# Two feed-forward layers on one NeuronCore: the second products as seven block products too

## What is computed

```
def hybrid_layer(...):            # first block, its last lines
    ...
    x + rms_norm(square(relu(rms_norm(x, g_pre_mlp) @ w_ff1)) @ w_ff2, g_post_mlp)

def swiglu(h, w1, w2):            # second block
    gt, up = jnp.split(h @ w1, 2, axis=-1)
    return (jax.nn.silu(gt) * up) @ w2
...
    h = rms_norm(x, norm_ffn_pre[l])
    x = x + rms_norm(swiglu(h, w_ffn_in[l], w_ffn_out[l]), norm_ffn_post[l])
```

## Time and profile before

| | us |
|---|---|
| median of 3 runs | 3385.32 (3380.46 to 3385.62) |
| the profiled execution's own time | 3380.83 |
| its span, first to last instruction | 3378.7 |
| TensorE busy | 3280.3 (97%) |
| VectorE busy | 1656.5 (49%) |
| ScalarE busy | 1066.0 (32%) |
| GpSimd busy | 1133.3 (34%) |
| chain that ended last, on TensorE | 85% of the span |

### The profile page before, as it was taken

How to read it: one execution, slowest core, us unless ns; L and a number is a source line. 1 busy time by engine, 2 the same in 40 slices (tenths; PEclk the granted TensorE clock), 3 DMA queues, 4 the chain that set the end, 5 groups by cost and what they waited for, 6 DMA issues and landing times.

```text
span 3378.7 us, 39689 instructions
## 1 busy us (share of the span) xinstructions
PE 3280.3 (97%) x15800; PEld 2669.5 (79%) x15800; DVE 1656.5 (49%) x2048; ACT 1066.0 (32%) x1479; POOL 1133.3 (34%) x667
## 2 busy tenths in 40 slices
PE   8999999999999999999999999999999999999997
PEld 6788777877876888788868778777778678887886
DVE  6752455435327675322153337563563577776213
ACT  3212444444324333211133333312343432223112
POOL 2112222212341554233322124341245345554325
PEclk9999999999999999999999999999999999999998
DMA  3545434316413223322224224224254222224223
GB/s 132 162 103 155 126 132 163 105 66 228 152 60 113 107 106 142 120 100 97 97 106 144 91 75 140 78 69 148 97 203 152 81 80 83 76 93 145 100 75 124
DMA packets 117198, 390.66 MB, mean 116 GB/s; under 512 B 13648, under 2 KB 23248, under 8 KB 116880
## 3 DMA queue, kind: packets, MB, share of 16 engines
q1 hardware_dynamic: 115984, 384.58, 33.3%
q10 hardware_dynamic: 1040, 3.67, 0.3%
HBM read 277.37 MB, written 113.84 MB: 116 GB/s over the span
## 4 chain that ended last, share of the span: by engine, by line
PE 85%; DVE 8%; issue 2%; ACT 2%; DMA 2%; POOL 1%; SPq 0%; DVEq 0%; POOLq 0%; ACTq 0%
PE pair L324 54%; PE pair L2145 16%; PE pair L443 4%; PE wide L834 2%; PE bank L654 2%; PE bank L802 2%; PE wide L567 1%; DVE act_lo L557 1%; DVE s_tmp L960 1%; POOL w_lo L2111 0%; PE wide L1513 0%; DVE p L625 0%; DMA proj<-p 0%; PE bank L1513 0%; DVE s_state L960 0%
## 5 line engine op out<-in xcount | busy, mean ns | idle before, releaser
L285 POOL TENSOR_TENSOR w_lo<-w_raw,w_hi 128x1024 fp32r<-128x1024 f32 (+1 forms) x240 | 564.8, 2358 | 1753.5 <-ACT w_hi L281 1712.8
L324 PE MATMUL pair<-act_hi,w_hi 128*128 128x512 f32 x2336 | 747.8, 401 | 10.4 <-DVE f1v L2170 6.1
L324 PE MATMUL pair<-act_lo,w_hi 128*128 128x512 f32 x2336 | 723.1, 391 | 0.0
L324 PE MATMUL pair<-act_hi,w_lo 128*128 128x512 f32 x2336 | 721.7, 390 | 0.0
L324 PEld LDWEIGHTS pair<-act_lo,w_hi 128*128 128x128 f32 x2336 | 439.2, 188 | 94.6
L324 PEld LDWEIGHTS pair<-act_hi,w_lo 128*128 128x128 f32 x2336 | 438.7, 188 | 94.7
L281 ACT CAST w_hi<-w_raw 128x1024 fp32r<-128x1024 f32 x210 | 220.7, 1051 | 909.9 <-PE pair L324 850.5
L324 PEld LDWEIGHTS pair<-act_hi,w_hi 128*128 128x128 f32 x2336 | 418.6, 189 | 92.0 <-issue 10.1
L625 DVE TENSOR_TENSOR p<-pair,rs 128x1024 f32<-128x1024 f32 x100 | 122.2, 1222 | 390.7 <-PE pair L324 390.6
L2298 DVE TENSOR_TENSOR f1acc<-f1acc,pair 128x1024 f32<-128x1024 f32 (+1 forms) x22 | 26.9, 1221 | 193.3 <-PE pair L324 193.3
L2111 POOL TENSOR_TENSOR w_lo<-w_raw,w_hi 128x512 fp32r<-128x512 f32 x64 | 98.7, 1544 | 60.2 <-ACT w_hi L2110 60.1
(11 more groups left out here) (627 smaller groups left out, 6192.8 us busy)
## 6 DMA issues: line engine op xcount, KB each, us to landing
w_raw<-in_stream SPq DMA_DIRECT2D x275, 512.0 KB, 3.6
proj<-p SPq DMA_DIRECT2D x101, 512.0 KB, 2.6
hidden<-f1v SPq DMA_DIRECT2D x32, 512.0 KB, 2.6
m2g<-proj SPq DMA_DIRECT2D x32, 512.0 KB, 5.0
act_lo<-hidden SPq DMA_DIRECT2D x24, 512.0 KB, 6.8
hidden<-f2v SPq DMA_DIRECT2D x22, 512.0 KB, 2.6
m1g<-proj SPq DMA_DIRECT2D x16, 512.0 KB, 3.5
f1hl<-hidden SPq DMA_DIRECT2D x16, 512.0 KB, 6.8
```

The lines of the kernel that those rows point to most:

```text
L285: last = nc.gpsimd.tensor_tensor(wlo[:, slot, at:at + n], raw[:, slot, at:at + n], whi[:, slot, at:at + n].bitcast(F32), ALU.subtract)
L324: last = nc.tensor.matmul(out_pair[:, h * HALF:(h + 1) * HALF], wt, a[:, h * HALF:(h + 1) * HALF], start=k == 0 and n_pass == 0, stop=k == ...
```

## The change

The second products are done in pairs of seven block products too, but for the last two output tiles of each layer. A pair of a second product is one of the four pairs of output tiles (i = 0 to 3) by one group of hidden tiles; the first layer gets 15 such pairs, the second 11 (the three of its last group have block products of 3 tiles, 9 matmuls, where the others have 12). The first products get one more pair in each layer, since only two units run plainly ahead of them, not four.

A block product takes one of eight "roles" of the activations: four are sums T1 to T4, four are plain blocks. For the hidden activations, `half_sums_of` makes the four sums on VectorE in SBUF for two hidden tiles at a time while the first product runs, and stores them to new DRAM buffers (`sums1`, `sums2`). At a change of group, each role is loaded into the place of the same role of the old group as soon as the last pair of the old group is through with it (`load_role`), in two pieces (j = 0 and 1) of two tiles each, 128x1024. `split_role` splits them: both high parts by ScalarE copies, the low part of piece 0 by VectorE, that of piece 1 by GpSimd. Roles 0 to 2 are split in the last three products of the old group's last pair, roles 3 to 6 in the first four products of the new group's first pair.

The seven products of a pair run in one order everywhere. Their results are summed in PSUM: ScalarE copies bank a into bank b ahead of product 2 and bank b into bank c ahead of product 4 (`seeds`), and the matmuls of products 2 to 6 accumulate onto what stands in their bank. The sums of weight blocks go to PSUM (`w_sum`), and four of the seven low parts of weights are VectorE's work now (`w_low`), three stay with GpSimd.

The diff's core ("..." marks what is left out):

```diff
-        pairs = pairs_in_all - 3
+        pairs = pairs_in_all - 2
...
-        S1, S2, S3, S4 = sq[:, H0], sq[:, H1], squares[:, H0], squares[:, H1]
+        sum_at = {4: wide[:, H0], 2: wide[:, H1], 1: bank[0][:], 6: bank[1][:]}
...
+        def weights_at(q, step):
...
+            elif step == 2:
+                w_high(q, 0)
+                w_low(q, 0)
+                w_sum(q, 1)
+                w_high(q, 1)
+            elif step == 3:
+                w_low(q, 1)
+                w_sum(q, 4)
+                w_sum(q, 2)
+                w_high(q, 2)
+                w_high(q, 3)
+                w_low(q, 3)
+            elif step == 4:
+                w_low(q, 2)
+                w_sum(q, 6)
+                w_high(q, 4)
...
+        def seeds(q, p):
+            if p == 0:
+                a_to_b[q] = A.mark(A.after(done[q, 0], b_read[q - 1] if q else entered[2]).copy(b, a))
+            elif p == 2:
+                b_to_c[q] = A.mark(A.after(done[q, 2], c_read[q - 1] if q else entered[1]).copy(c, b))
...
+        def outer(q, p):
...
+            if p == 1:
...
+                d_mid[q] = into(r1[:, H1], d, 1, True)
+            elif p == 2:
+                V.after(b_to_c[q])
+                b_read[q] = into(r1[:, H0], b, 2, True)
+            elif p == 3:
+                a_read[q] = into(r0[:, H0], a, 3, True)
+            elif p == 4:
+                c_mid[q] = into(r1[:, H1], c, 4, False)
...
+        def split_role(g, n, mark=None):
...
+            for j in range(2):
...
+                m = A.mark(A.after(here[g, n, j], mark).copy(hi, src))
+                on = G if j else V
+                role_ready[g, n, j] = on.mark(on.after(m).tensor_tensor(lo, src, hi.bitcast(F32), ALU.subtract))
...
+            for p in range(7):
+                product(q, p)
+                seeds(q, p)
+                if changing is not None and p not in waiting:
+                    load_role(changing, p, done[q, p])
...
+                (inner if q < pairs else outer)(q, p)
...
+                if changing is not None:
+                    if p > 3:
+                        split_role(changing, p - 4)
+                if opened is not None and p < 4:
+                    split_role(opened, p + 3, done[q - 1, 6])
...
+                if q < last:
+                    weights_at(q + 1, p)
...
+        PE.after(a_read[last], b_read[last], c_read[last], d_read[last])
```

More of the change, by code:

```diff
@@ L2016, in mlp @@
-        weights, sums = {}, {}
+            b_ready[i, k] = V.mark(V.after(high).tensor_tensor(operand(hl, (i,), k), t_src[i](k),
+                                                               operand(hh, (i,), k).bitcast(F32), ALU.subtract))
+        first = base + 2
+        n_groups = len(groups)
+        total = pairs + 4 * n_groups - 1
+        last = total - 1
+        first_m = [sum(groups[:g]) // 2 for g in range(n_groups)]
+        a, b, c, d = (pair[at][:, half] for at in range(2) for half in (H0, H1))
@@ new lines, in w_fetch @@
+        def w_fetch(q):
+            for n in range(2):
+                u = first + 2 * q + n
+                fetch_unit(u + 2, u % 2)
+        def weights_at(q, step):
+            if step == 0 and q > 1:
+                w_low(q - 1, 6)
+            elif step == 2:
[14 more added lines that the diff above has]
+                w_high(q, 4)
+            elif step == 5:
+                w_low(q, 4)
+                w_high(q, 5)
+                w_low(q, 5)
+                G.then(sums_of[q, 6])
+                nc.gpsimd.sem_inc(s_split, 2)
+                nc.scalar.sem_inc(s_whi, 2)
+            elif step == 6:
+                w_high(q, 6)
+                w_fetch(q)
@@ L2054, in mlp @@
         for k in range(4):
[L2055 to L2069 removed]
+            t_low(T2, k, high[T2, k])
@@ new lines, in outer, with into @@
+        def outer(q, p):
+            g, i = group_of(q), (q - pairs) % 4
+            r0, r1 = y[:, 2 * i, :], y[:, 2 * i + 1, :]
+            def into(dst, psum, n, fresh):
+                V.after(done[q, n])
+                if fresh and g == 0:
+                    return V.mark(nc.vector.tensor_copy(dst, psum))
+                return V.mark(V.then().tensor_tensor(dst, dst, psum, ALU.add))
+            if p == 1:
+                if g == 0 and i == 1:
+                    V.after(*(s.last() for s in hid_out))
+                if g == 0 and i == 3:
+                    V.after(hid_sum.last())
+                d_mid[q] = into(r1[:, H1], d, 1, True)
```

612 lines of the change are left out of this document (346 added, 266 removed).

## The result

| | before | after |
|---|---|---|
| median | 3382.91 us (7 runs) | 3394.68 us (7 runs, 3393.15 to 3397.26) |
| ratio to before | | 1.0037, 95% interval 1.0025 to 1.0048 |
| span of the profiled execution | 3378.7 us | 3391.8 us |
| granted clock of TensorE, mean | 0.993 | 0.984 |

The account below looks back on a forecast made before the run. TensorE, busy 97% of the span, bounds the kernel through its number of matmuls. 3380.8 - 74.1 (matmuls) - 31 (stops) + 81 (changes) + 8 (entries) + 2 + 2 (ends) = 3368.7, stated as 3370 us; range 3312 to 3425.

Parts of the forecast that it names:

- Matmuls and old stops: Both feed-forward layers: 327 fewer matmuls, 74.1 us less, and 31 us of TensorE stops taken out.
- entries: Start of each layer: late bank of product 1 and late second seed, 4 us each, 8 in all.
- The mechanism of a change: At a change of group VectorE and GpSimd exclude each other, delaying evictions TensorE needs; changes cost 81 us in all.
- locked work: Role pieces, weight steps and sums at a change that exclude each other: 29.5 us without a gap, until 25.6.
- the time of `c_mid`: New group's first pair: eviction of product 4 ends at 24.7, product 6 due at 21.7, so waits 3.0.
- full change: Change of group, three in the first layer, one in the second: 8.4 us of waits plus 1.9 of clock, 10.3 each.
- the short one: Change into the second layer's last group, with smaller pieces: wait for `c_mid` 5.2 with 1.9 of clock, 7 us.
- The two first changes: Each layer's change out of the first product, with more work in front: 14.4, with the clock 16.3, twice: 33 us.
- the clock after the last stop 1.9: Lower TensorE clock behind a change's last stop, 1.9 us; that after the stop of 3.1 is called hidden.
- last groups and tails: Layer ends: tails wait 0.9 each for the last eviction, 2 us; squares 0.6 in three second-layer pairs, 2 us.
- Rival 1: Changes of group are covered by kinder ordering or lock, 4 us each: 3316 us; chance 0.22.
- Rival 2: Seeds hold up product 2 in each of 34 first-product pairs, 1.5 us each, 51 more: 3421 us; chance 0.23.

Follow-up runs that it names:

- e2: Changed kernel with GpSimd's seven subtractions per change of group left out (those tiles keep their unsplit value, work the result needs): 3330.0 us, 0.9845 of before.
- e5: Changed kernel with twenty matmuls nobody reads filling the stop ahead of product 6 in each new group's first pair: 3379.61 us, 0.9991 of before.
- e1: Changed kernel with next-pair weight steps moved behind the eviction of product 4 in a group's first pair: 3373.71 us, 0.9974 of before.
- e11: Changed kernel with the second square of a last-group pair issued at product 1 of the next pair: 3387.21 us, 1.0013 of before.
- e8: Changed kernel with weight steps 2 and 3 behind product 4's eviction and each role split one product earlier: 3365.72 us, 0.9945 of before.
- e13: e12 with role 0's split behind product 4's eviction in the last pair of a group that opens a further one: 3357.38 us, 0.9928 of before.
- e3: Changed kernel with both pieces of each role split by VectorE, none by GpSimd: 3389.82 us, 1.0023 of before.
- e9: e8 with both pieces of roles 1, 3 and 5 on VectorE: 3387.31 us, 1.0012 of before.
- e12: e8 with the edit of e11, and the earlier role split only at changes between two groups: 3358.56 us, 0.9927 of before.

## Why the prediction was wrong

**Matmuls and old stops.** 74.1 and 31 us were taken out, as stated: TensorE is busy for 44 us less though its clock stands lower, and the stops of the earlier trace rows are gone; what the entries cost now is counted below.

**The mechanism of a change was right.** The forecast had the locked work end 25.6 us after the nominal start of the new pair. That start is 1527.0 in the change shown, and GpSimd's last piece ends at 1551.6, the sum held up behind it at 1552.2, so 25.2. The last and longest stop ends with `c_mid`, as said, and the two kinds of step hold each other up, as said. e2 shows that it is GpSimd's pieces; that they do it through the lock follows for the last stop from the sums of 2.68 and 2.12 us that are 0.70 without them. The loads hid, as stated, though 6 times 1.05 MB in 13.6 us is 463 GB/s and not 440: none of ScalarE's copies of a role (L2448) waited for one. The Trainium skill, "SBUF — State Buffer", "SBUF: two separate sides", says that whichever of the two starts first keeps the port pair for its whole instruction; the 2.68 and 2.12 us above agree, and so does the eviction L2376, which reads PSUM with one input and stays at 0.69 throughout.

**The first step that failed: the time of `c_mid`; changes 91 for 81.** The sum let this eviction end 24.7 us after the start of the pair, and TensorE be 8.4 late there. It ends at 1553.7, 26.7 after the start, and product 6 is 10.5 late. The rows show the 2 us. Role 6's piece on VectorE ends at 22.4, not 21.3, since ScalarE's copies of that role stand behind a weight copy that waits for the held-up sum L2100. What follows it takes 4.3 us, not 3.4, since L2102 is held up behind GpSimd's last piece. So a full change costs 12.55 to 12.8 for 10.3 and the short one 9.3 for 7. The two first changes were slightly too high in the sum (16.3 against 15.5 and 15.9). Inside the sum errors cancelled too: the last stop is 5.4, not 3.0, while those at products 3 to 5 (1.9 together) did not come. Such a playing-through of queues is fair for the sum of a change and not for each stop.

**The clock was not what failed.** The sum had it once per change, "the clock after the last stop 1.9", and said that the one after product 2's stop is hidden. Thirteen falls came at changes where seven were counted, but the last one of a change costs 2.1 us in the first layer, and the others are hidden: e5 and e1 have full changes with and without the fall behind product 2, and product 6 starts equally late in both (16.79 and 16.82 us, 13.29 and 13.30). In the first changes it is the same. The seed of product 2 ends 4.8 us later than in an undisturbed pair in both layers. In the second layer TensorE waits 2.1 us for it (1.9 in the sum); in the first the clock falls behind product 1's stop, and TensorE needs that time for its matmuls. Product 6 is 13.4 late in both.

**The second: entries, 16 for 8.** Product 1 waits 2.2 us at each entry (1.3 in the sum), and in the first layer the clock falls behind it. The late seed of the sum (1.7, the second one) did not come; the first late ones are those of the third pair, 0.85 and 1.00, and in the first layer the fourth pair's, 1.85, behind an eviction that is 1.37 late. The second layer has two more stops, 1.34 and 0.94. None of these had a term; the prediction took a pair's seeds at nothing, from its steady state. Why the queues run late up to the fourth pair no run here shows.

**The third: last groups and tails, 10.4 for 4.** The tails wait 0.93 each, as stated. The squares were charged 0.6 in each of three pairs of the second layer. What was missed is that the second square waits for the addition of the first (the one buffer `sq`): a stop of 3.3 us and 3.1 of slow clock behind it in the second layer, a seed 1.2 late in the first. e11 gives 7.5, which is all of it.

**What is left.** 10 + 8 + 6 is the whole miss of 24 us, and it alone turned the sign. The stops that the waits list add up to 76 of the 117 us and the fifteen falls to 31. Most of the other 10 is in how a stop is listed: from the end of the matmul before it, which is 0.39 long, where without a stop the next one starts after 0.23. That is 0.16 more for each of the 37 stops, 6 us, and the second matmul behind a stop comes some 0.08 to 0.11 late as well, 3 us.

**Rivals.** Rival 1 (changes covered, 3316) did not come. e2 shows what it would take, GpSimd's pieces gone altogether, and even then 3330. Rival 2 (seeds late in every pair) did not come either, although the kernel is slower: past the first pairs they are 19.04 us apart in both layers, and in the first ScalarE waits for TensorE ahead of each seed (timeline of ScalarE, after; against the earlier trace rows):

```profile
1216.25 0.57 ACT L2264 COPY pair<-pair 128x512 f32<-128x512 f32 x1 [0.46 <-PE pair L2253]
...
1235.29 0.57 ACT L2264 COPY pair<-pair 128x512 f32<-128x512 f32 x1 [0.46 <-PE pair L2253]
```

So the slower side was given 0.26 for the wrong reason. The forecast's own bounds (57 to 103 for the changes) held 91; what lacked was a case in which the small terms, entries and ends, are wrong together. All three were counted low; entries and ends were priced from one wait and not from the queue it stands in. The range of 3312 to 3425 held the time.

**What the experiments add.** The gain in matmuls was not lost to one wait. It is spent at seven changes on an amount of work that VectorE and GpSimd can't do together in the length of one pair, and at the ends of the layers on queues in another order than the steady one. Moving the work earlier, later or over to the other engine (e8, e13, e3, e9) mostly moves the stop. What was won came from order: no eviction that TensorE waits for behind work for the next pair (21 us in e1), the pieces earlier (8 more in e8), the squares apart (7).

## What to carry to other kernels

Where a change trades matmuls for work on VectorE and GpSimd, add up the work that excludes each other in the stretch where it falls, and charge a stop of TensorE of about 2 us or more with the clock behind it, 1.7 to 3.1 us here. But leave that out where another engine's queue sets when a later stop ends: there the slow clock cost nothing. In VectorE's queue an eviction that TensorE waits for goes ahead of preparation for later, above all ahead of steps with both inputs in SBUF. First and last pairs are not the steady state: play their queues through by themselves.

## What the runs showed of the hardware

- A stop of 1.9 to 2.5 us was followed in most places by the lower clock, but not in all. The same stop of product 1 at the first change was 2.34 us in e13 with the clock at 0.5 behind it, and 2.33 us in e12 with no fall. A stop of 2.90 us in e12 (at 3139) had none either, nor had the 1.35 in e2 and the 1.73 in e12.
- Such a fall slowed TensorE's matmuls by 1.7 to 3.1 us. Behind product 2's stop it delayed nothing, since the queues of GpSimd and VectorE set when TensorE could go on (16.79 against 16.82 us in e5, 13.29 against 13.30 in e1).
- GpSimd's subtraction of 128x1024 takes 2.40 us alone and up to 3.4 with VectorE's beside it; VectorE's 128x512 sum 0.70 alone and up to 2.68 under GpSimd's. The two take turns, and a queue of both runs without a gap: GpSimd was busy for the whole 4.00 us of the stretches at 1537 and 1541.
